# An encoder layer on one core: where the residual's scaled sum is written, and in which order the last block's output projection and last down units run

## The reference, cut to what matters

```python
h = _rmsnorm(x, g_pre_mix) * (1 + sc1) + sh1
proj = h @ w_in                                   # 17 blocks of 128 columns
# pooling, conformer convolution and short convolution over time, on proj
mix = jnp.concatenate([ya, yb, yc], axis=-1) @ w_out
x = x + gt1 * _rmsnorm(mix, g_post_mix)           # residual, kind "mix"
h = _rmsnorm(x, g_pre_ffn) * (1 + sc2) + sh2
f = (jax.nn.silu(h @ w_gate) * (h @ w_up)) @ w_down   # 2816 hidden, 22 blocks of 128
x = x + gt2 * _rmsnorm(f, g_post_ffn)             # residual, kind "ffn"
```

## Time and profile before

| | us |
|---|---|
| three runs, median | 2392.24 |
| lowest and highest | 2386.87, 2393.14 |
| the profiled execution, its own time | 2390.17 |
| its span, first to last instruction | 2388.4 |
| TensorE busy | 2325.7 (97%) |
| VectorE busy | 1341.3 (56%) |
| ScalarE busy | 1029.7 (43%) |
| DMA | 361.62 MB, mean 151 GB/s |

### The profile page before, as it was taken

The page is one execution under the profiler, slowest core; times in us unless marked ns, Lnnn a source line. Parts: engine busy times, 40 slices in busy tenths (PEclk is TensorE's granted clock), DMA queues, the critical chain, the costliest instruction groups (busy, mean ns, idle before and its releaser), DMA issues.

```text
span 2388.4 us, 30206 instructions
## 1 busy us (share of the span) xinstructions
PE 2325.7 (97%) x12452; PEld 2102.2 (88%) x12452; DVE 1341.3 (56%) x1917; ACT 1029.7 (43%) x1433; POOL 37.1 (2%) x78
## 2 busy tenths in 40 slices
PE   8999998999999999999999999999999998999997
PEld 2848898897999898899999899989889997899986
DVE  1775796479643467744357763436784434443343
ACT  2434555545353444435353435344443424432332
POOL 0000000000000000000000000000000000000000
PEclk9999999999999999999999999999999999999999
DMA  8664463355433353353344344335335433434332
GB/s 308 221 210 158 154 217 134 131 176 172 163 142 124 124 176 130 129 183 124 124 150 159 123 168 143 131 120 180 123 115 176 123 125 107 177 134 165 124 132 79
DMA packets 101742, 361.62 MB, mean 151 GB/s; under 512 B 12260, under 2 KB 14436, under 8 KB 101605
## 3 DMA queue, kind: packets, MB, share of 16 engines
q1 hardware_dynamic: 101606, 359.70, 43.3%
HBM read 340.73 MB, written 18.93 MB: 151 GB/s over the span
## 4 chain that ended last, share of the span: by engine, by line
PE 91%; DVE 5%; DMA 2%; ACT 1%; issue 1%; POOL 0%; SPq 0%; DVEq 0%; POOLq 0%; ACTq 0%
PE ps L464 90%; DVE wlo L1032 2%; DVE pr L1153 1%; PE ps L506 1%; DMA raw<-in_w_gu 1%; ACT junk L729 1%; DVE xr L1100 0%; DMA gate<-in_gpost 0%; DMA raw<-in_w_mix 0%; DVE g_lo L1081 0%; DVE h_lo L1074 0%; POOL rstd_m L984 0%; DVE ps L1092 0%; DMA raw<-in_w_ada 0%; DVE pr L1175 0%
## 5 line engine op out<-in xcount | busy, mean ns | idle before, releaser
L464 PE MATMUL ps<-h_hi,whi 128*128 128x384 f32 (+1 forms) x2928 | 962.7, 329 | 17.7 <-DVE xr L1100 14.2
L464 PE MATMUL ps<-h_hi,wlo 128*128 128x384 f32 (+1 forms) x2928 | 958.4, 327 | 0.0
L464 PE MATMUL ps<-h_lo,whi 128*128 128x384 f32 (+1 forms) x2928 | 958.1, 327 | 0.0
L1032 DVE TENSOR_TENSOR wlo<-raw,whi 128x1024 fp32r<-128x1024 f32 x546 | 664.3, 1221 | 521.1 <-ACT whi L690 510.4
L690 ACT ACTIVATE whi<-raw 128x1024 fp32r<-128x1024 f32 x546 | 576.7, 1057 | 803.7 <-DMA raw<-in_w_gu 539.0
L464 PEld LDWEIGHTS ps<-h_hi,whi 128*128 128x128 f32 x2928 | 555.3, 190 | 25.6 <-DVE xr L1100 15.8
L464 PEld LDWEIGHTS ps<-h_lo,whi 128*128 128x128 f32 x2928 | 554.9, 190 | 1.8
L464 PEld LDWEIGHTS ps<-h_hi,wlo 128*128 128x128 f32 x2928 | 554.8, 189 | 0.0
L1153 DVE SCALAR_TENSOR_TENSOR pr<-u,col,pr 128x384 f32<-128x384 f32 x450 | 259.5, 612 | 1.2
L464 PE MATMUL ps<-whi,g_hi 128*128 128x512 f32 x748 | 236.0, 397 | 8.1 <-DVE xr L1100 7.1
L464 PE MATMUL ps<-wlo,g_hi 128*128 128x512 f32 x748 | 231.5, 391 | 0.0
(11 more groups left out here) (110 smaller groups left out, 1154.8 us busy)
## 6 DMA issues: line engine op xcount, KB each, us to landing
raw<-in_w_gu SPq DMA_DIRECT2D x264, 512.0 KB, 3.2
raw<-in_w_mix SPq DMA_DIRECT2D x150, 512.0 KB, 3.3
raw<-in_w_dn SPq DMA_DIRECT2D x132, 512.0 KB, 3.2
raw<-in_w_ada SPq DMA_DIRECT2D x48, 512.0 KB, 4.4
xt<-in_x_all SPq DMA_DIRECT2D x17, 512.0 KB, 6.0
xr<-in_x_all SPq DMA_DIRECT2D x17, 512.0 KB, 5.8
xr<-x_all SPq DMA_DIRECT2D x17, 512.0 KB, 5.8
x_all<-xr SPq DMA_DIRECT2D x5, 1536.0 KB, 7.5
```

The costliest lines, as they stand in the source:

```text
L464: return nc.tensor.matmul(out, lhsT, rhs, start=start, stop=stop, skip_group_check=True)
L1032: tt(wlo[:, s, :], raw[:, s, :], whi[:, s, :].bitcast(F32), ALU.subtract).then_inc(w_lo, 1)
```

## The change

The scaled sum of every residual is written to `xt` in SBUF, and TensorE waits for that write (new semaphore mix_read) in place of the addition. Squares and residual of "ffn" are put in front of the two `ahead` of gate/up m = 0. In the last block, tile 0 of the output projection gathers in banks 0 and 1, its tiles are squared and scaled in the order 1, 2, 0, and down units 0 to 2 run tile by tile, three units for a tile before the next tile. The last down projection takes tile 2 first, its last three units run tile by tile as well, and each tile is squared, scaled, added and stored when it is done (new semaphore tile_done). The diff, without the declarations, the renaming of `mix_ps` in `ada_out`, a new return path in `rstd`, blank lines and the removed body of `by_rows`, `mix_out` and `down`; in VectorE's stream `residual("ffn", c - 1)` moves in front of `ahead` just as `mix_squares` does in ScalarE's:

```diff
@@ -144,7 +145,9 @@
 
 def tile_order(r):
     kind, b = RES[r]
-    return [0, 1] if NT[b] == 2 else [0, 1, 2] if kind == "mix" else [2, 0, 1]
+    if NT[b] == 2:
+        return [0, 1]
+    return [2, 0, 1] if kind == "ffn" else [1, 2, 0] if b == NB - 1 else [0, 1, 2]
 
 
 def res_tile(r, t):
@@ -314,8 +318,12 @@
             kind, j = HIGH[Y[i]]
             return y_pr[:, SLOT[kind] + j, :]
 
-        def mix_ps(t):
-            return ps[:, 2 + 2 * t:4 + 2 * t, :].rearrange("p a n -> p (a n)")
+        def sum_bank(r, t):
+            return 0 if r == RES.index(("mix", NB - 1)) and t == 0 else 2 + 2 * t
+        def bank_pair(bank):
+            return ps[:, bank:bank + 2, :].rearrange("p a n -> p (a n)")
 
         def gu_bank(m, i):
             return (6 if m % 2 else 0) + i
@@ -437,6 +445,8 @@
                         load("gu", c, m, i)
                     if m == 4 and c + 2 < NB:
                         sp.wait_ge(t_full, KD * (norm("F", c) + 1))
+                        if c:
+                            sp.wait_ge(res_tiles, res_all(RES.index(("ffn", c - 1))))
                         load_x(c + 2)
                     if m == 7 and c:
                         store(y_v, "ffn", c - 1)
@@ -529,38 +539,61 @@
                 wait_split(n)
                 by_columns(n, ps[:, j % 2, 0:w], q, w, j == 0)
 
+            def by_rows(r, tiles, units, before=None):
+                for t in tiles:
+                    for n, high, low, first, end, parts, count in units:
+                        s, c, bank = n % RING, slice(t * P, (t + 1) * P), sum_bank(r, t)
+                        if first and before is not None:
+                            before(t)
+                        if t == tiles[0]:
+                            pe.wait_ge(parts, count)
+                            wait_split(n)
+                        for st, mv, one, two in ((high, whi, first, False), (high, wlo, False, False),
+                                                 (low, whi, False, end)):
+                            for h in range(2):
+                                w = slice(512 * h, 512 * h + 512)
+                                last = mm(ps[:, bank + h, :], st[:, c], mv[:, s, w], one, two)
+                        if t == tiles[-1]:
+                            last.then_inc(w_used, 1)
+                        elif end and r == len(RES) - 1:
+                            last.then_inc(tile_done, 1)
 
             def mix_out(c, k):
                 n, r = UNIT["out", c, k], RES.index(("mix", c))
                 if k == 0 and c == 0:
                     pe.wait_ge(gates_made, 4)
+                def before(t):
+                    if r and t < NT[RES[r - 1][1]]:
+                        pe.wait_ge(mix_read, res_tile(r - 1, t))
+                    if c and t == TB - 1:
+                        pe.wait_ge(silu_ready, ff_count(c - 1, NF - 1))
+                        pe.wait_ge(g_ready, ff_count(c - 1, NF - 1))
+                    elif c == NB - 1 and t == 0:
+                        pe.wait_ge(silu_ready, ff_count(c - 1, NF - 2))
+                        pe.wait_ge(g_ready, ff_count(c - 1, NF - 2))
+                by_rows(r, range(NT[c]), [(n, y_high(k), y_low(k), k == 0, k == NMIX - 1, y_lo_ready, NMIX * c + k + 1)],
+                        before)
+            def down(b, ks):
+                r, units = RES.index(("ffn", b)), []
+                for k in ks:
+                    at = NF * b + k
+                    units.append((UNIT["dn", b, k], g_hi[:, at % G_RING, :], g_lo[:, at % G_RING, :], k == 0, k == NF - 1,
+                                  g_lo_ready, at + 1))
+                def before(t):
+                    if t < NT[RES[r - 1][1]] and sum_bank(r - 1, t) == sum_bank(r, t):
+                        pe.wait_ge(mix_read, res_tile(r - 1, t))
+                    if t == TB - 1:
+                        pe.wait_ge(silu_ready, ff_count(b, NF - 1))
+                        pe.wait_ge(g_ready, ff_count(b, NF - 1))
+                by_rows(r, tile_order(r) if b == NB - 1 else range(NT[b]), units, before)
 
             def gate_up(b, m):
                 q, w = norm("F", b), NT[b] * P
@@ -571,8 +604,7 @@
                     elif m == 0:
                         pe.wait_ge(t_read, KD * q + KD - 1 + i)
                     elif i == 0:
-                        pe.wait_ge(res_tiles, res_tile(RES.index(("ffn", b - 1)), NT[b - 1] - 1) if b
-                                   else res_all(0))
+                        pe.wait_ge(mix_read, res_tile(RES.index(("ffn", b - 1)), NT[b - 1] - 1) if b else res_all(0))
                     wait_split(n)
                     by_columns(n, ps[:, gu_bank(m, i), 0:w], q, w, m == 0 and i == 0)
 
@@ -663,7 +695,10 @@
                         transposes(norm("F", 0), ch)
                 else:
                     for k in range(NF):
-                        down(c - 1, k)
+                        if c < NB - 1 or k >= G_RING:
+                            down(c - 1, [k])
+                        elif k == 0:
+                            down(c - 1, range(G_RING))
                         ch = (k - 6) // 2
                         if k >= 6 and k % 2 == 0 and ch < KD:
                             if ch == 0 and c + 1 < NB:
@@ -671,14 +706,15 @@
                             transposes(norm("F", c), ch)
                 for m in range(NF):
                     if c + 1 < NB and m == STATS_AT[c]:
-                        pe.wait_ge(res_tiles, res_all(RES.index(("ffn", c - 1)) if c else 0))
+                        pe.wait_ge(mix_read, res_all(RES.index(("ffn", c - 1)) if c else 0))
                         for i in range(3):
                             statistics(c + 1, i)
                     if c + 1 < NB and m == STATS_AT[c] + 3:
                         statistics(c + 1, 3)
                     gate_up(c, m)
-            for k in range(NF):
-                down(NB - 1, k)
+            for k in range(NF - G_RING):
+                down(NB - 1, [k])
+            down(NB - 1, range(NF - G_RING, NF))
 
@@ -722,12 +758,15 @@
 
             def mix_squares(kind, b):
                 r = RES.index((kind, b))
-                act.wait_ge(w_used, UNIT[("out", b, NMIX - 1) if kind == "mix" else ("dn", b, NF - 1)] + 1)
                 for i, t in enumerate(tile_order(r)):
+                    if r == len(RES) - 1 and i < NT[b] - 1:
+                        act.wait_ge(tile_done, i + 1)
+                    else:
+                        act.wait_ge(w_used, UNIT[("out", b, NMIX - 1) if kind == "mix" else ("dn", b, NF - 1)] + 1)
                     if tiles_before_res(r) + i:
                         act.wait_ge(mix_ssq, tiles_before_res(r) + i)
-                    nc.scalar.activation(junk[:, :], mix_ps(t), ACT.Square, scale=D ** -0.5, accum_out=ssq_m[:, t:t + 1])\
-                        .then_inc(mix_ssq, 1)
+                    nc.scalar.activation(junk[:, :], bank_pair(sum_bank(r, t)), ACT.Square, scale=D ** -0.5,
+                                         accum_out=ssq_m[:, t:t + 1]).then_inc(mix_ssq, 1)
 
             def modulate(q, k):
                 kind, b = NORMS[q]
@@ -934,10 +973,10 @@
                             modulate(norm("F", c), ch)
                             h_split(norm("F", c), ch)
                 for m in range(NF):
+                    if c and m == 0:
+                        mix_squares("ffn", c - 1)
                     for i in range(2):
                         ahead("gu", c, m, i)
-                    if c and m == 0:
-                        mix_squares("ffn", c - 1)
                     act.wait_ge(w_used, UNIT["gu", c, m, 0] + 1)
                     if m >= 2:
                         act.wait_ge(g_ready, ff_count(c, m - 2))
@@ -991,12 +1033,21 @@
 
             def mix_rstds(kind, b):
                 r = RES.index((kind, b))
-                first = tile_order(r)[0]
+                order = tile_order(r)
                 pool.wait_ge(mix_ssq, tiles_before_res(r) + 1)
-                rstd(ssq_m, rstd_m, first, first + 1, mix_rstd)
-                pool.wait_ge(mix_ssq, res_all(r))
-                rest = (1, NT[b]) if first == 0 else (0, first)
-                rstd(ssq_m, rstd_m, *rest, mix_rstd)
+                rstd(ssq_m, rstd_m, order[0], order[0] + 1, mix_rstd)
+                if r == len(RES) - 1:
+                    for i, t in enumerate(order[1:]):
+                        pool.wait_ge(mix_ssq, tiles_before_res(r) + i + 2)
+                        rstd(ssq_m, rstd_m, t, t + 1, mix_rstd)
+                else:
+                    pool.wait_ge(mix_ssq, res_all(r))
+                    lo, hi = min(order[1:]), max(order[1:])
+                    if hi - lo == len(order) - 2:
+                        rstd(ssq_m, rstd_m, lo, hi + 1, mix_rstd)
+                    else:
+                        rstd(ssq_m, rstd_m, lo, lo + 1, None)
+                        rstd(ssq_m, rstd_m, hi, hi + 1, mix_rstd)
 
```

(63 more changed lines are left out.)

3 lines of the change are left out of this document (1 added, 2 removed).

## The result

The changed kernel takes 2370.55 us (median of four runs, 2368.96 to 2373.41); the kernel before, run beside it, 2392.69. The ratio is 0.9914, with a 95% interval of 0.9901 to 0.9928: faster by 0.9%, 22 us, where 2369 us were forecast. The profiled execution's own time is 2368.96 and its span 2367.2, 21.2 less than before.

What follows compares the result with a forecast made beforehand. TensorE, busy 97% of the span, was taken as the bound. Terms -14.16 - 6.81 + 2.84 + 0.4 + 0.3 + 0.85 - 5.9 = -22.5 us gave 2367.7 or 2369.7, stated as 2369; range 2362 to 2377.

Steps and rivals of the forecast that it cites:

- The five boundaries: Block boundaries before gate/up (1,0): all five TensorE idle stretches go, -14.16 us, and the low clock behind four, -6.81.
- rival (a): Block boundaries: stretches go but low clock stays as costly; -15.7 us, 2376; chance 0.15.
- Cover of the splits: Weight splits of gate/up (2,0) and (2,1), now behind the residual: 3.8 us to spare, so they cost nothing.
- (c): Block boundaries: splits behind the residual replace the wait if 4.5 us later; no change, about 2388; chance 0.03.
- (d): Block boundaries: residual holds VectorE over 10 us more per block; slower, time passes 2397; chance 0.03.
- The last output projection and the group: Last output projection and down units 0 to 2 tile by tile: 9.9 us stall on unit 2's g_lo; stage +3.5 us.
- Rival (b): Down units 0 to 2: unit 2's g_lo doesn't hold the group; 7.09 and 2.07 us vanish, -35, 2356; chance 0.05.
- Rival (e): Down group costs more than 3.5 us, say 10, as ScalarE's queue makes units 4 to 6 late; 2375; chance 0.08.
- The three small terms: Last output projection's stage: +2.84 us net for the longer stall, +0.4 low clock, +0.3 for units behind the group.
- The start of the last down projection: Last down projection starts with tile 2, whose banks wait for g_f of m=21: +0.85 us.
- The tail: Behind the last matmul only one tile is left; the last addition ends at +4.5 instead of +10.4 us: -5.9.
- the 3.3 us of the last store stay: End of the tail: the last store's 3.3 us behind the last addition were taken as unchanged.

Runs made afterwards that it cites:

- the wait alone: Changed kernel with ffn squares and residual back behind the two gate/up m = 0 weight splits, TensorE still waiting for the scaled sum: 2370.63 us, ratio 0.9915.
- the run with unit 2's halves early: Changed kernel with both hidden-value halves of block 4's down unit 2 made during the last output projection, before the residual; group kept: 2357.62 us, ratio 0.9858.
- one by one: Changed kernel with block 4's down units 0 to 2 run singly again, tile 0 of the projection still in banks 0 and 1: 2360.14 us, ratio 0.9874.
- the run with the tail undone: Changed kernel with the last down projection as before: tiles 0, 1, 2, single units, squares and residual after the last unit: 2374.42 us, ratio 0.9928.
- the run with six more operations: Changed kernel with six unused VectorE operations before the last addition of each ffn residual but the last, 7.5 us in all: 2386.20 us, ratio 0.9978.
- the run with three more operations: Changed kernel with three unused VectorE operations, about 1.25 us each, before the last addition of each ffn residual but the last: 2368.02 us, ratio 0.9899.

## Why the prediction was right

**The five boundaries**: -20.97 forecast, -21.9 measured. The mechanism is shown from three sides: the stretches are gone in the trace, either half of the change removes them (the wait alone all but 0.88 us in one block), and a longer residual brings them back at another unit. The low clock went with the stretches, in every block where it had stood behind one; rival (a) is out. It was right to count it: it is a third of this gain. Each boundary brought 0.1 to 0.3 us more than its stretch and its low clock before; the cause of that is open.

**Cover of the splits**: 3.8 us forecast, 4.8 measured. The step mis-sized was the moment when unit (2,0) is ready: I took the end of both splits (+12.9) where the first one's end counts (+11.7). Rivals (c) and (d) needed more than this cover, and no row gave it. Rival (c)'s price was worked out wrongly: 4.5 us lost at five places is 22.5, against 21.0 won there and 1.5 in the other stages, so no change, 2390 to 2392, and not 2388.

**The last output projection and the group**: the stall was forecast at 9.9 us, ended by g_lo, and was 10.08; the stage +3.5 and was +3.3. Rival (b) is out by this stall, whose cause the run with unit 2's halves early shows. Rival (e), units 4 to 6 late enough to cost 10 us, is out as well: units 4 and 5 each began about 0.25 us late (the first is the row at 2007.44: 0.69 behind the pair before it, where 0.45 is usual), 0.5 where 0.3 was forecast. The three small terms (0.4 of clock, 0.3 for the units behind, 2.84) can't be told apart well: the window behind the stall, against the earlier trace rows,

```profile
1991.90:1996.60 4.70, 4.61 (x14) 3.68 (x15) 1.17 (x2) 0.00 (x0) 0.00 (x0) 0.65 0.01 3
```

lost (1 - 0.65) x 4.70 = 1.6 us to the low clock where 2.07 went before, so -0.4 in place of +0.4, the low end of its bounds. That is one draw of several: in the other six traces with this 10.1 us stretch 1.5 to 2.8 us were lost behind it (in that of the changed kernel again 0.61 over 6.00 us, 2.3). What the prediction didn't see is that the same stage would have been 7.7 us better without the group (one by one, 145.6 us against 153.3). It compared the change with before, not with its own parts.

**The start of the last down projection**: +0.85 forecast, 0.88 of stretch, +1.1 in the matmuls' starts.

**The tail**: -5.9 forecast, -5.0 measured. The last addition ended 10.4 us behind the last matmul before and ends 4.6 behind it now (2363.10 against 2358.49), -5.8. The mis-sized step is "the 3.3 us of the last store stay": they became 4.1.

**The first block**: +1.2 us that no step of the prediction has. Changed there are only the destination of the scaled sums and TensorE's waits for them. The window from 362 to 376 us, before, after, and in the run with the tail undone:

```profile
362.00:376.00 14.00, 8.72 (x41) 6.31 (x42) 8.89 (x19) 1.58 (x3) 0.00 (x0) 0.76 0.07 29
```

```profile
362.00:376.00 14.00, 9.04 (x28) 5.50 (x29) 9.31 (x20) 1.44 (x2) 0.00 (x0) 0.63 0.02 8
```

```profile
362.00:376.00 14.00, 8.99 (x43) 6.65 (x44) 8.63 (x18) 1.97 (x5) 0.00 (x0) 0.76 0.08 30
```

(1 - clock) x 14 is 3.4 us of lost clock before and 5.2 after. The run with the tail undone has the changed code in this block and 3.4 as before. Of the twelve traces with the changed code here, that one and the run with six more operations lost 3.4 us, the other ten 4.9 to 5.2, all around idle time that this block has anyway (in both traces statistics waiting for VectorE). Matmul 2429 begins between 447.6 and 451.6 us in the twelve, at 450.0 in the one trace before. So +1.2 lies within what the same code gives from one execution to the next, and no cost of the change is shown. That the change leaves the odds of the longer low clock alone is not shown either, with one trace of the kernel before.

The span missed the forecast by 1.3 us: -0.9 at the boundaries, +1.2 in the first block, -0.2 in the group, +0.25 and +0.9 at the last two steps. The order of events was right at every step; that the sum is this close is in part luck, as the two largest misses on the slow side, the first block and the tail, stand against the boundaries' 0.9 on the other.

## What to carry to other kernels

When several operations stand in one engine's order, look for a short one that the bound engine waits for, and ask what is in front of it: here 0.55 us of work behind a residual cost 10 us, and moving it gained about half of what the whole change had gained, or a little more (10.6 us by the stage, 12 to 13 by the medians). Cost each part of a change against the version without it, not only the whole against before; parts that remove the same wait twice, or that lose what another wins, don't show in the sum. And where the bound engine stands for 2 to 3 us, look at its clock behind the stretch: it cost another 1.7 us each time it fell here.

## What the runs showed of the hardware

**The low clock behind a short stretch is not fixed by its length.** Behind stretches of 2.7 to 3.1 us TensorE fell to 1.2 GHz four times in five before; with six more operations two in four, and not behind 1.53 us. It fell behind 3.50 us and both times behind 2.15 in the runs told above, and not behind 1.71 and 1.23. Each fall behind a stretch of these lengths lost 1.6 to 1.7 us. So one trace gives the price of a fall, and only several give how often it comes.

**The end of the program came in two lengths, 1 us apart.** The view of the queues from 2358 us to the end, after the change, and below it for the run with three more operations:

```profile
DMA packets 289, 1.06 MB, mean 114 GB/s; under 512 B 32, under 2 KB 32, under 8 KB 288
...
q1 hardware_dynamic: 288, 1.05, 28.3%
q14 instruction: 1, 0.01, 0.2%
```

```profile
DMA packets 288, 1.05 MB, mean 126 GB/s; under 512 B 32, under 2 KB 32, under 8 KB 288
...
q1 hardware_dynamic: 288, 1.05, 31.1%
```

After the change one packet of the instruction queue runs 2.0 us behind the last addition, and the span ends 4.1 us behind that addition. So it is in all ten traces with such a packet (4.0 to 4.2 us); in the three without one, the kernel before and the two with more operations, it is 3.1 to 3.3. This is the 0.8 us by which the tail's last term was mis-sized. That the packet is the cause is not shown: no run changes the length of the code alone.

**An addition of 1024 columns costs VectorE the same from SBUF as from PSUM**: 1.218 us on average after, 1.213 before. By an estimate from the two fixed costs that the Trainium skill gives (VectorE: DVE Perf Modes, The TRN2 errata; 58 cycles for a source in SBUF, 120 for one in PSUM) it would be 0.065 us shorter; these rows don't show that.
